# Prompt attention: value products spread over the steps by key tile, turns eight steps behind the scores, four pairs written out straight

## The reference

```python
# FoX: keys up to the query, with a bias of summed log forget values
s = jnp.einsum('bqhd,bkhd->bhqk', qb, k) * scale + cb[..., :, None] - c[..., None, :]
p, _ = softmax_stats(s, kpos[None, :] <= qpos[:, None])
o = jnp.einsum('bhqk,bkhd->bqhd', p, v)
# windows: three groups (128, 1), (512, 4), (2048, 16); each has own q, k, v
a = jax.nn.softmax(jnp.stack(lses, 0), axis=0)
o = jnp.einsum('gbsh,gbshd->bshd', a, jnp.stack(outs, 0))
```

## Times and profile before

| what | us |
|---|---|
| median of 3 runs | 1907.22 (1904.94 to 1908.43) |
| the profiled execution | 1906.57 |
| its span | 1904.8 |
| prompt attention in it, from its first score to the start of the closing stage | 1137.29 to 1360.47 |
| closing stage | 1360.47 to the end |

### The profile page before, as it was taken

The page is one execution under the profiler, slowest core; times in us unless marked ns, Lnnn a source line. Parts: engine busy times, 40 slices in busy tenths (PEclk is TensorE's granted clock), DMA queues, the critical chain, the costliest instruction groups (busy, mean ns, idle before and its releaser), DMA issues. The chain is left out here.

```text
span 1904.8 us, 33016 instructions
## 1 busy us (share of the span) xinstructions
PE 1752.0 (92%) x10749; PEld 1553.1 (82%) x10749; DVE 1093.7 (57%) x2474; ACT 957.0 (50%) x1644; POOL 871.8 (46%) x508
## 2 busy tenths in 40 slices
PE   7999999999599999999999968878799899999998
PEld 5787787899588888888888846767697889989897
DVE  5745546421387787888887876667452442424251
ACT  5434343332267777777777767677422322223130
POOL 1514333300137778778687647465233233333331
PEclk9999999999799999999999987989899999999999
DMA  6354362633699999999999879453445366566652
GB/s 222 90 173 130 110 192 97 205 109 107 185 339 335 321 330 340 329 329 333 337 340 316 279 232 312 132 161 113 139 132 220 133 264 242 224 261 264 242 222 114
DMA packets 226029, 426.70 MB, mean 224 GB/s; under 512 B 24457, under 2 KB 85770, under 8 KB 224466
## 3 DMA queue, kind: packets, MB, share of 16 engines
q1 hardware_dynamic: 222706, 422.63, 66.5%
q0 software_dynamic: 3168, 2.11, 0.5%
HBM read 392.36 MB, written 119.59 MB: 269 GB/s over the span
## 5 line engine op out<-in xcount | busy, mean ns | idle before, releaser
L1024 POOL TENSOR_TENSOR vv_lo<-v_raw,vv_hi 128x1024 fp32r<-128x1024 f32 x178 | 400.4, 2256 | 165.2 <-ACT vv_hi L1090 159.1
L1844 POOL TENSOR_TENSOR w_lo<-w_raw,w_hi 128x2048 fp32r<-128x2048 f32 x39 | 180.7, 4633 | 338.7 <-ACT w_hi L1859 338.7
L1082 ACT ACTIVATE kt_hi<-ktp 128x1024 fp32r<-128x1024 f32 (+1 forms) x192 | 186.5, 971 | 111.7 <-PE ktp L1253 108.7
L1108 DVE TENSOR_TENSOR kt_lo<-ktp,kt_hi 128x1024 fp32r<-128x1024 f32 (+1 forms) x192 | 220.8, 1150 | 10.0 <-ACT kt_hi L1082 8.1
L1253 PE MATMUL ktp<-ident,k_raw 128*128 128x128 f32 x1440 | 194.0, 277 | 19.2 <-DMA k_raw<-in_cache_fox_k 18.4
L1269 PE MATMUL s_ps<-kt_hi,q_st 128*128 128x256 f32 (+3 forms) x768 | 207.5, 303 | 0.4 <-DVE mx_parts L1148 0.4
L1253 PEld LDWEIGHTS ktp<-ident,k_raw 128*128 128x128 f32 x1440 | 168.7, 143 | 47.2 <-DMA k_raw<-in_cache_fox_k 24.0
L663 PE MATMUL acc<-w_hi,xn_hi 128*128 128x512 f32 x480 | 194.7, 406 | 2.4 <-POOL w_lo L302 2.4
L1090 ACT ACTIVATE vv_hi<-v_raw 128x1024 fp32r<-128x1024 f32 (+1 forms) x192 | 191.6, 998 | 4.9 <-PE o_ps L1285 4.5
L1269 PE MATMUL s_ps<-kt_lo,q_st 128*128 128x256 f32 (+3 forms) x768 | 192.6, 284 | 0.0
L663 PE MATMUL acc<-w_lo,xn_hi 128*128 128x512 f32 x480 | 190.4, 397 | 0.0
(11 more groups left out here) (243 smaller groups left out, 4209.2 us busy)
## 6 DMA issues: line engine op xcount, KB each, us to landing
k_raw<-in_cache_fox_k SPq DMA_DIRECT2D x256, 256.0 KB, 7.0
v_raw<-in_cache_fox_v SPq DMA_DIRECT2D x256, 256.0 KB, 5.8
out_win_kv_sample<-in_cache_win_kv SPq DMA_DIRECT2D x32, 2040.0 KB, 9.7
w_raw<-in_w_in SPq DMA_DIRECT2D x32, 1024.0 KB, 5.8
k_raw<-in_cache_win_kv SPq DMA_DIRECT2D x40, 512.0 KB, 10.5
v_raw<-in_cache_win_kv SPq DMA_DIRECT2D x40, 512.0 KB, 11.6
w_raw<-in_w_up SPq DMA_DIRECT2D x16, 1024.0 KB, 5.5
w_raw<-in_w_down SPq DMA_DIRECT2D x16, 1024.0 KB, 5.0
```

The costliest lines, as they stand in the source:

```text
L1024: gp.tensor_tensor(vv_lo[:, slot, 0:tiles, :], v_raw[:, i % RAW_RING, 0:tiles, :], vv_hi[:, slot, 0:tiles, :].bitcast(F32), ALU.subtract). ...
L1082: act.activation(kt_hi[:, slot, :, 0:n], ktp[:, i % 2, :, 0:n], ACT.Copy).then_inc(k_hi, 1)
L1108: ve.tensor_tensor(kt_lo[:, slot, :, 0:n], ktp[:, i % 2, :, 0:n], kt_hi[:, slot, :, 0:n].bitcast(F32), ALU.subtract).then_inc(k_lo, 1)
L1844: gp.tensor_tensor(w_lo[:, slot, :], w_raw[:, slot, :], w_hi[:, slot, :].bitcast(F32), ALU.subtract).then_inc(slab_lo_done, 1)
```

## The change

Three things change, all in `attend_prompt`.

- The loop goes. `straight` writes all 128 steps and the ones behind them out, with the pair's number a constant, where `stream` had a loop.
- The lags. Turns are at 24 (they were at 28), `turns_lo` at 25. The value splits move from 27 and 28 to 35 (ACT) and 36 (POOL).
- `weigh` is no longer one job of twelve products. `weigh(kt)` does the three products of one key tile, at lags 26, 30, 34 and 38 for key tiles 0 to 3. Each step from 38 on holds one such job. `outputs` is at lag 39 (it was at 31).

The semaphore `weighed` counts jobs of three products now, starts at 32, and is waited for by number of the chunk. ACT's value split waits for the product job one step before it, `turns_hi` for one two steps before.

```diff
-TURN_BEHIND, LOW_BEHIND, WEIGH_BEHIND, COPY_BEHIND = 28, 29, 30, 31
-Q_AT, K_AT, V_AT = (0, 18), 13, 27
+TURN_BEHIND, LOW_BEHIND, WEIGH_BEHIND = 24, 25, 26
+WEIGH_STEP = 4
+COPY_BEHIND = WEIGH_BEHIND + 3 * WEIGH_STEP + 1
+Q_AT, K_AT = (0, 18), 13
+V_HI_BEHIND, V_LO_BEHIND = 35, 36
...
-                j = i - V_AT
-                if 0 <= j < SETS:
-                    s = SET_ORDER[j]
-                    gp.wait_ge(v_split_hi, pieces(p, j))
+
+            def values_lo(p, i):
+                if i < SETS:
+                    s = SET_ORDER[i]
+                    gp.wait_ge(v_split_hi, pieces(p, i))
                     gp.tensor_tensor(v_lo[:, s], v_raw[:, s], v_hi[:, s].bitcast(F32), ALU.subtract).then_inc(v_split, 1)
...
-            stream(gp, PAIRS, CHUNKS, (0, diagonals), (RECIP_BEHIND, normalise), (1, split_lo))
+            straight(PAIRS, CHUNKS, (0, diagonals), (RECIP_BEHIND, normalise), (1, split_lo), (V_LO_BEHIND, values_lo))
...
                     act.wait_ge(v_in, 16 * SETS * (p + 1))
-                    if not first:
-                        act.wait_ge(weighed, JOBS * p - SETS + j + 1)
+                    done(act, weighed, at_chunk(p, i) - SETS)
...
-                if qt == 0:
-                    act.wait_ge(weighed, JOBS * p + SETS * hh + i % 4 + 1 - SETS if not isinstance(p, int) else max(0, JOBS * p + SETS * hh + i % 4 + 1 - SETS))
+                done(act, weighed, at_chunk(p, i) - CHUNKS // 2)
                 done(act, turned, at_chunk(p, i))
...
-                act.wait_ge(weighed, JOBS * p + SETS * hh + i % 4 + 1)
+                done(act, weighed, at_chunk(p, i))
...
-                lots = []
-                for kt in range(Q_TILES):
+            def weigh(kt):
+                def tile_products(p, i):
...
+                    if hh == 0 and kt == 0:
+                        pe.wait_ge(v_split, pieces(p, i % 4))
+                    if i % 4 < 2 and kt == 0:
+                        pe.wait_ge(o_copied, 4 * p + 2 * hh + kind + 1)
+                    done(pe, turned_lo, at_chunk(p, i))
...
+                    for n, (v, x) in enumerate(((v_hi, pt_hi), (v_lo, pt_hi), (v_hi, pt_lo))):
+                        last = pe.matmul(o_ps[:, kind, cols], v[:, s, kt, :], x[:, at + kt * P:at + end * P], start=(i % 4 < 2 and kt == 0 and n == 0),
+                                         stop=(unit_ends(i) and kt == Q_TILES - 1 and n == 2))
+                    last.then_inc(weighed, 1)
+
+                return WEIGH_BEHIND + kt * WEIGH_STEP, tile_products
+
+            pe.sem_inc(weighed, CHUNKS)
+            straight(PAIRS, CHUNKS, (SCORE_BEHIND, score), (TURN_BEHIND, turn), *(weigh(kt) for kt in range(Q_TILES)))
```

More of the change, by code:

```diff
@@ L1376, in attend_prompt @@
         UNITS = CHUNKS // 2
-        JOBS = 2 * SETS
         def hold(eng):
@@ L1558, in split_inputs, with values_hi @@
                     act.activation(k_hi[:, s], k_raw[:, s], ACT.Copy).then_inc(k_split_hi, 1)
-                j = i - V_AT
-                if 0 <= j < SETS:
-                    s = SET_ORDER[j]
+            def values_hi(p, i):
+                if i < SETS:
+                    s = SET_ORDER[i]
                     act.wait_ge(v_in, 16 * SETS * (p + 1))
-                    if not first:
-                        act.wait_ge(weighed, JOBS * p - SETS + j + 1)
+                    done(act, weighed, at_chunk(p, i) - SETS)
                     act.activation(v_hi[:, s], v_raw[:, s], ACT.Copy).then_inc(v_split_hi, 1)
@@ L1593, in outputs @@
                 kind, rows = chunk_kind(i), slice(64 * hh, 64 * hh + 64)
-                act.wait_ge(weighed, JOBS * p + SETS * hh + i % 4 + 1)
+                done(act, weighed, at_chunk(p, i))
                 dst = o_all[rows, bass.ds(p + kind * PAIRS, 1), 0:SEQ].rearrange("p a n -> p (a n)")
                 act.activation(dst, o_ps[rows, kind, :], ACT.Copy).then_inc(o_copied, 1)
-            stream(act, PAIRS, CHUNKS, (EXP_P_BEHIND, exponentials), (NORM_BEHIND, normalise), (TURN_BEHIND, turns_hi), (COPY_BEHIND, outputs), (0, split_inputs))
+            straight(PAIRS, CHUNKS, (EXP_P_BEHIND, exponentials), (NORM_BEHIND, normalise), (TURN_BEHIND, turns_hi), (COPY_BEHIND, outputs), (0, split_inputs), (V_HI_BEHIND, values_hi))
         @block.vector
@@ L1661, in turns_lo @@
                                  turned_part(pt_hi, i).bitcast(F32), ALU.subtract).then_inc(turned_lo, 1)
-            stream(ve, PAIRS, CHUNKS, (KEEP_BEHIND, keep), (KEEP_BEHIND, maximum), (RECIP_BEHIND, denominators),
+            straight(PAIRS, CHUNKS, (KEEP_BEHIND, keep), (KEEP_BEHIND, maximum), (RECIP_BEHIND, denominators),
                    (LOW_BEHIND, turns_lo), (1, queries_lo))
@@ L1698, in turn @@
                 last.then_inc(turned, 1)
[L1700 to L1710, removed]
-                lots = []
-                for kt in range(Q_TILES):
-                    end = min(kt + 2, Q_TILES) if s == 1 else Q_TILES
[L1714 to L1719, removed]
@@ L1721, in _ @@
-            stream(pe, PAIRS, CHUNKS, (SCORE_BEHIND, score), (TURN_BEHIND, turn), (WEIGH_BEHIND, weigh))
+            def weigh(kt):
+                def tile_products(p, i):
+                    hh, qt, s = chunk(i)
+                    kind = chunk_kind(i)
+                    if qt < Q_TILES - 1:
+                        return
+                    if hh == 0 and kt == 0:
[3 more added lines that the diff above has]
+                    done(pe, turned_lo, at_chunk(p, i))
+                    hold(pe)
+                    end = min(kt + 2, Q_TILES) if s == 1 else Q_TILES
+                    cols, at = slice(kt * P, end * P), pt_at[s] + kt * pt_step[s]
+                    for n, (v, x) in enumerate(((v_hi, pt_hi), (v_lo, pt_hi), (v_hi, pt_lo))):
[3 more added lines that the diff above has]
+                return WEIGH_BEHIND + kt * WEIGH_STEP, tile_products
```

## The result

The changed kernel takes 1887.02 us in the median of four runs (1886.23 to 1890.64), the kernel before 1906.62 beside it (1904.94 to 1908.43). The ratio is 0.9898, with a 95% interval from 0.9882 to 0.9914: 19.6 us faster. I had said 1898. The direction was right and the range held the time, but the gain is more than twice the one forecast, so the working has to be gone through for what it missed.

A forecast was written before the change was run, and what follows sets the result against it. No engine was taken as full; the bound changes within a pair, and the end of prompt attention sets the total. Step 143 at 1333.7 plus 17.1 gave 1350.8, 9.7 earlier, taken as 9: 1898 us, 8-in-10 range 1879 to 1911.

The forecast's parts named there:

- Part 1: Loop removed: PE's 9.8 us of pauses at steps 64 and 96 go; a pair without one 49.6 us, straight code free.
- Part 2: Products spread over steps: a pair takes 49.7 us, the same as 49.6 without the pause, since splits lose the burst's cover.
- Seven steps bound by ACT: Steps 0 to 6 and 16 to 22 of a pair: ACT's work at 90%, 14.2 and 12.1 us.
- the stretches bound by PE: Steps 7 to 15 and 23 to 31 of a pair: PE's 10.7 us at 92%, so 11.7 each.
- the last half: Steps 128 to 143, no queries split: 11.4 us for 128 to 134, then 10.4 for eight more steps.
- Part 3: First pair: POOL still waits for the bias until 1179.16; step 48 at 1187.4 against 1185.19, step 64 at 1212.5.
- steps 48 to 54 at the slower level: First pair: 12.4 us of PE work at prices times 1.8, so 13.4 us for these steps.
- Spreading pays too: Rival: the 2.9 pairs from step 55 take 41.7 us each, 23 us more gained; 1872 to 1888, chance 0.22.
- The order locks: Rival: PE waits some 3 us a pair for the value-split chain, or fetches cost 5 us; 1903 to 1911, chance 0.20.
- PE's clock falls: Rival: without bursts PE stays longer at 1.2 GHz, a pair up to 60 us; 1911 to 1935, chance 0.12.

The follow-up runs named there:

- e1: The kernel before with the loop written out straight and nothing else changed; 1896.56 us, ratio 0.9947.
- p1: The kernel before, loop kept, with 85 semaphore increments added on DVE at the start of an earlier stage; 1898.94 us, ratio 0.9972.
- e4: The changed kernel with its first two pairs written out and a loop over the last two, one jump at step 96; 1886.87 us, ratio 0.9904.
- e2: e1 with the turns and what hangs on them four steps earlier, products still in bursts; 1896.59 us, ratio 0.9950.
- e3: The changed kernel with turns, products and value splits four steps later, turns at lag 28; 1886.08 us, ratio 0.9904.
- f1: The changed kernel with the value rests on DVE instead of POOL, same lag; 1882.96 us, ratio 0.9895.
- x1: e3 with the first pair's value splits alone back at lags 27 and 28, ahead of POOL's mask; 1880.20 us, ratio 0.9876.
- x2: x1 with a pair's window copies issued behind the next pair's loads instead of ahead of them; 1872.88 us, ratio 0.9838.

## Why the prediction was right and wrong

The end of the stage came at 1341.4 where I had 1350.8. The 9.4 us between, term by term (forecast and measured length; the closing stage by ACT's first instruction):

| stretch | forecast | measured | missed |
|---|---|---|---|
| start of the stage | 1137.29 | 1135.82 | 1.5 |
| 16-48 | 50.1 | 48.24 | 1.9 |
| 48-64 | 25.1 | 22.61 | 2.5 |
| 64-96 | 49.7 | 50.09 | -0.4 |
| 96-128 | 49.7 | 47.95 | 1.7 |
| 128-143 | 21.8 | 19.16 | 2.6 |
| 143 to the closing stage | 17.1 | 17.55 | -0.4 |

**Part 1 was right.** The pauses were worth 8.9 us (e1; 7.9 in the stage), and I had up to 9.8. A pair without one takes 50.8 where I had 49.6, and straight code cost no visible fetch in DVE's waits. The reason was incomplete: not the jump costs 5 us but the load of code behind it, which a shift of 85 instructions removes (p1) and the loop of e4, with as many steps in its body but at another place of the code, doesn't have.

**Part 2, "spreading is neutral", is the step that failed.** I put its worth at nothing. It is worth about 9.7 us by the medians (e4 against e2, with the same turns, on the same chip), of which the two profiles show 6.9 in the stage and the rest ahead of it, where the code is the same; the changed kernel's stage is 8.0 us under e2's. So it is somewhat under half of the gain in the stage. The total that I took for a pair was nearly right, but by errors that cancel. Seven steps bound by ACT were priced at ACT's work over 90%, with half of its exponentials and scalings, 6.6 us, in them. Measured, ACT was 96 to 99% busy in steps 64 to 70 and 128 to 134 (such shares stood in the earlier trace rows already, 7.94 of 8.12 us in steps 98 to 105), and 89% in 80 to 86, about as priced. The larger error is the 6.6. What is left of its busy time after the splits and copies that I had named is 12.19 - 6.24 = 5.95 us in steps 64 to 70, 9.34 - 4.35 = 4.99 in 80 to 86 and 8.30 - 3.72 = 4.58 in 128 to 134, not 6.6. The forecast for these three was 14.2, 12.1 and 11.4 us; they took 12.31, 10.51 and 8.63. Against that, the stretches bound by PE, forecast 11.7, took 14.93 and 12.34 in one pair and 13.63 and 11.92 in the next, since PE's clock there was 0.84 to 1.00 and not 1.00 throughout, and the first of each pair also holds a wait of PE at the next first score, 1.72 and 1.35 us. In the last half no query splits come, and none of that second error: there 2.6 us were missed. It was also the place to look twice beforehand. The forecast of 21.8 for it was longer than the 21.0 of before, though a burst of PE went and only some 2 us of ACT's work came (all four value splits fall behind step 128 now, where before had one of them).

**Part 3.** The mechanism was right: POOL waits for the bias, and its mask starts at 1176.92 (about 1179 forecast, less the 1.5 of the earlier start). What failed is the term "steps 48 to 54 at the slower level", 13.4 us. They took 10.71 with the granted clock at 1.00; PE's busy time was 8.43, not 12.4. I had carried the slower level over from the kernel before, where the clock in these steps is 0.50. This term alone is 2.7 us, and the whole first pair (16 to 64) 4.4 of the 9.4 missed, more than the pairs (1.3) or the last half (2.6): the sum by parts was off most where I took the slower clock for given.

**The rivals.** *Spreading pays too* is the nearest. Its mechanism happened, and 1887.0 is at the slow end of its times (1872 to 1888), but with a pair of 48 to 50 rather than 41.7. What kept it from more fits what I held against it: value splits, output copies and query splits fall together on ACT at this lag. Four steps later the value splits lie in steps 7 to 10 of the next pair, behind its first query splits, and a pair is 44.9 (e3). That the splits alone do it isn't shown, since e3 moves the turns as well. *The order locks* happened in a small way as well. Two waits of 3.4 us came once a pair, named POOL's value rest, and were priced right at 3 us each. They were hardly a loss, since ACT was full in the same steps: with POOL relieved (f1) a pair falls by 2.2 and 0.1 us, and PE waits for DVE instead. Even the 2.2 may not be POOL's: e4 keeps the waits for `v_lo`, and both its pairs take 48.3. *PE's clock falls* didn't happen. The pairs had 0.90 and 0.96 (before 0.91), and 1.00 at the later lag; steps 80 to 86, at 0.60 before, had 0.99. The Trainium skill ("TensorE: Matmul & The Clock Gate", A second HAM failure mode: psum-queue depth-cycling) tells of short idles between groups that make the clock swing. The clock does swing in both kernels, but the spreading, with its short idles, didn't make it slower.

Not settled: why the pair 64-96 has a lower clock (0.90) and takes 2.1 us more than the next one (0.96) with the same code and the same waits for `v_lo`. By these shares PE was at 1.2 GHz for some 10 us of the one and 4 of the other; at half speed the 6 us between would cost up to 3 (my estimate), enough for the 2.1. And the 1.5 us ahead of the stage I can only show as scatter between kernels whose code there is the same.

## What to carry to other kernels

When bursts of one engine are spread, ask of every stretch which engine is full, take its own work there from the trace by instruction and not as a share of the pair, and price it near its full length where that engine is the bound (96 to 99% busy here); then ask what lost its cover, because what the spread work collides with decides most of its gain (here 0.7 to 2.9 us a pair under e1 at one lag, 5.9 at a lag four steps later). Treat the first round apart from the steady ones: it has other waits. Small loads ahead of large copies were worth 8.1 us in it, about as much as the loop. The early values brought 6.4, but only against e3, which had made them late; with them in place, the spreading at the later lag takes 16.3 us off the stage of e1 (x1), where the changed kernel takes off 9.7. And before a loop is blamed for its jumps, shift its code by some instructions.

## What the runs showed of the hardware

- A jump back cost about 5 us at one place of the code and nothing to be seen at three others (85 and 170 instructions on, and in e4's loop). Where it cost, queue q14 loaded code around the jump; in p1 it loaded none from 1214 to 1300, with both jumps in that stretch.
- ACT was 99% busy over 12.3 us (steps 64 to 70), though what it works on comes from PE and DVE step by step. Queues that depend on each other left it next to no gaps.
- Kernels with the products spread had a granted clock of 0.90 to 1.00 over a pair: 1.00 where PE's longest wait was about 1.6 us (e3), 0.93 with one of 2.79 (f1), 0.90 and 0.96 with one of 3.4 (the changed kernel). The longest wait isn't all: e1, with bursts, had 0.97 and 0.90 with none over 1.4 us. What causes what isn't shown.
- Copies that are issued ahead of a row of 256 KB held that row back by 10 us (12.42 in e3), although no engine's work in the stage needs the copies; issuing them behind the next pair's loads was worth 8.1 us of the first pair (x1 to x2).
- A wait that the profile calls "issue" can be one for another engine. PE's of 1.72 us at 1233.91 ends when POOL is through with its first key rest, which had queued behind a scaling; in e4 the wait at the same place, 1.57 us, is named `POOL k_lo`:

```profile
1233.91 0.30 PE L1686 MATMUL s_ps<-k_hi,q_hi 128*128 128x128 f32 x1 [1.72 <-issue]
```

```profile
1230.69 1.89 POOL L1511 TENSOR_TENSOR probs<-probs,r_den 128x1024 f32<-128x1024 f32 x1 [3.99 <-DVE r_den L1656]
1232.54 2.50 POOL L1498 TENSOR_TENSOR k_lo<-qk_raw,k_hi 128x512 fp32r<-128x512 f32 x2
```
